# Constant matmuls at seven borders of a two-block network on one core, and one half of a weight split placed earlier

## The chip, the cores and the metric

The program runs on one core of a Trainium2 chip. The metric is device time in microseconds (us). Engines are named as in the profile: PE (TensorE, with PEld for its weight loads), DVE (VectorE), ACT (ScalarE), POOL (GpSimd), and SP, which issues the weight loads from memory. PE is granted one of two clocks, 2.4 or 1.2 GHz; the profile writes them as 1.00 and 0.50.

## The reference, cut to what matters

256 tokens of width 1024 go through a gated mixer block, a squared-relu feed forward, an RMS norm, and then two layers of a second block, each with gated feed forwards, an attention or a pooling mixer, and a layer norm after each part. All is float32. What this case touches is the norm between one part and the next:

```python
def rms_norm(x, w=None):
    xf = x.astype(jnp.float32)
    y = xf * lax.rsqrt(jnp.mean(jnp.square(xf), axis=-1, keepdims=True) + EPS)
...
def layer_norm(x, g, b):
    xf = x.astype(jnp.float32)
    mu = jnp.mean(xf, axis=-1, keepdims=True)
    var = jnp.mean(jnp.square(xf - mu), axis=-1, keepdims=True)
    y = (xf - mu) * lax.rsqrt(var + LN_EPS)
    return (y * g.astype(jnp.float32) + b.astype(jnp.float32)).astype(x.dtype)
...
    for i in range(DEPTH_2):
        x = layer_norm(DEEPNORM_ALPHA * x + 0.5 * swiglu(x, ffn_w_gu[i, 0], ffn_w_down[i, 0]), ...)
        ... y = moba_attention(x) or pool_mixer(x) ...
        x = layer_norm(DEEPNORM_ALPHA * x + y, ln_g[i, 1], ln_b[i, 1])
        x = layer_norm(DEEPNORM_ALPHA * x + 0.5 * swiglu(x, ffn_w_gu[i, 1], ffn_w_down[i, 1]), ...)
```

## The kernel before, in words

Activations lie transposed: 8 blocks of 128 channels by 256 tokens (`XS`, whose first half is called `xb` and holds x, and whose second half `sq` holds its squares). Each product is computed in three matmuls of a rounded format: the activation and the weight are each cut into a rounded part and a rest (`hi` and `lo`), and PE adds lo x hi, hi x lo and hi x hi (lines 601, 603 and 604 of the profile). `H` holds both parts of the normed x, one block of `H` is one step of the sum over channels.

Weights stream in panels of 128 x 2048 floats (1 MB), in the order in which they are used. SP loads a panel into one of four `raw` places. ACT copies each half of it, rounded, into `w_hi` (line 1104), and DVE subtracts it into `w_lo` (line 1504). These two together are called the split of a half panel. `w_hi` and `w_lo` have two places, so the split of a half waits until PE is through with the same half of the panel two before (`half_used`).

The program is written out per engine, in a fixed order; semaphores tie the engines. After the first, interwoven part come 17 stages, from `out` to `down3`. Eight of them end in a norm (`NORMED`): `out`, `ff2`, `down0`, `att_out`, `down1`, `down2`, `pool_out`, `down3`. What lies between such a stage and the first product of the next one is called a border here; seven have a next stage. At a border:

- The last four output banks are finished one by one. DVE takes each into x (`new_x`, line 1560, or 1565 where there is no mean), ACT squares it (1112), and DVE and POOL fold the blocks into `part` (1573, 567).
- PE sums over channels with a matrix of constant 1/1024 (`stats`, lines 747 to 757), mean first, then squares. ACT squares the mean (1174), DVE forms the variance (1618, 1619, or 1621 where there is no mean), ACT takes logarithm and exponential (1177, 1179), which gives the inverse root.
- Then for each of the 8 blocks: DVE subtracts the mean (`centred`, 1608), multiplies by the scale and the inverse root (`scaled`, 1636), ACT rounds it into `H` (1188, 1186), and DVE writes the rest (`lo`, 1644, 1642), which raises `norm_lo`.
- PE's next stage begins with its first group, 96 matmuls over 8 blocks: twelve for a block, which it may do as soon as that block's `norm_lo` is there (`ready`).

Two halves of the second panel of the next stage are split inside the border (`split_after`). Half 0: on ACT ahead of the logarithm, on DVE in `apply_norm` at m = 3, between the second block's rest and the fourth block's scaling. Half 1: on ACT after the fourth rounding, on DVE at m = 5.

Of the kernel before, what the change touches and what calls it, by code (L numbers as in the profile page):

```python
# [10 lines left out]
P = 128  # L11
T = 256
TT = T // P
D = 1024
KD = D // P
CHUNK = 512
PANEL = 4 * CHUNK
BANKS = 4
# [153 lines left out]
def two_blocks(nc, panels, x_in, c_in, cols_in, heads_in, ws_in, bs_in, wdt_in, rel_in, onehot_in, inv_in,  # L172
               skew, out):
    ctx = ExitStack()
    with ctx:
# [416 lines left out]
        def _(pe):  # L592
# [169 lines left out]

            def bias_rows(first, n):

                for h in range(first, first + n):
                    if h >= 2:
                        pe.wait_ge(S["rev_other" if h % 2 else "rev_copied"], h // 2)
                    to = banks[:, 1 + h % 2, :]
                    pe.matmul(to, rel_r[:, 0, h:h + 1].to_broadcast([33, P]), onehot_r[:, :], start=True, stop=False)
                    pe.matmul(to, rel_r[:, 1, h:h + 1].to_broadcast([33, P]), onehot_r[:, :], start=False, stop=True)\  # L770
                        .then_inc(S["rev_done"], 1)
# [203 lines left out]
            stats(2, False, "out")  # L975
            stage_k8("ff1", H, norm_block(1))
            stage_long("ff2", HH, 32, operand_of("ff1", 4))
            stats(3, False, "ff2")

            norm = [4]  # L980

            def feed_forward(i):
                stage_k8(f"gu{i}", H, norm_block(norm[0] - 2))
                stage_long(f"down{i}", HH, 22, operand_of(f"gu{i}", 2))
                stats(norm[0], True, f"down{i}")
                norm[0] += 1
# [80 lines left out]
            stats(norm[0], True, "att_out")  # L1067
            norm[0] += 1
# [4 lines left out]
            s = INDEX["pool_group"]  # L1073
# [16 lines left out]
            stats(norm[0], True, "pool_out")  # L1090
            norm[0] += 1
# [4 lines left out]
        def _(act):  # L1096
# [52 lines left out]
            def squares_post(s, g, G):  # L1149
                if by_bank(s, g):  # L1150
                    act.preload_act_table_set("natural_log_exp_and_others")
                    for b in range(BANKS):
                        square(s, g, b)
                    return
                act.wait_ge(taken, FIRST_GROUP[s] + g + 1)
                act.activation(by_group(sq)[:, g, :, :], by_group(xb)[:, g, :, :], ACT.Square)\
                    .then_inc(S["squares"], BANKS)
# [12 lines left out]
            def border_root(n, mean, stage_name):  # L1170
# [4 lines left out]
                split_after(split, stage_name, 0)  # L1175
# [309 lines left out]
        def _(vec):  # L1485
# [89 lines left out]
            def last_group(name, g, G, new_x):  # L1575

                for b in range(BANKS):
# [3 lines left out]
                    bank_post(INDEX[name], g, G, b, new_x)  # L1581

# [47 lines left out]
            def apply_norm(k, dest, scale, bias, stage_name, mean=False, operand=True):  # L1630
# [21 lines left out]
                for m in range(KD + 1):  # L1652
                    if m in (3, 5):
                        split_after(split, stage_name, m // 2 - 1)
# [490 lines left out]
```

## Time and profile before

| what | value |
|---|---|
| time, median of 3 runs | 1671.67 us (1669.38 to 1672.41) |
| the profiled execution: its own time | 1670.81 us |
| its span, first to last instruction | 1668.9 us |
| granted PE clock, mean | 0.968 |
| PE busy | 1584.6 us (95%) |
| DVE busy | 997.2 us (60%) |
| ACT busy | 770.9 us (46%) |
| POOL busy | 185.7 us (11%) |
| DMA queues, mean | 174 GB/s |

The span is 1.9 us shorter than the execution's own time, so what is read inside the span is set against 1670.81 and not against the median. A busy share of PE is not the share of its peak: matmuls overlap in the record, and at the lower clock PE is just as busy with half the work.

### The profile page before, as it was taken

How to read it: one execution, taken by the hardware profiler on the slowest of the kernel's cores; microseconds unless marked ns; L12 is line 12 of the kernel's file. 1: busy time of each engine (PE TensorE's matmuls, PEld its weight loads, DVE VectorE, ACT ScalarE, POOL GpSimd, SP SyncE). 2: the span in 40 equal slices, each digit the busy share in tenths (PEclk: the TensorE clock that was granted, in tenths of full speed). 3: DMA queues.
4: the chain of work that ended last, by engine and by line, in shares of the span. 5: the costliest groups of instructions: out<-in, count | busy, mean ns of one | idle time of the engine just before them, and what ended most of it. 6: DMA issues, size and time to landing. Idle time of an engine off the chain costs nothing.

```text
span 1668.9 us, 30136 instructions
## 1 busy us (share of the span) xinstructions
PE 1584.6 (95%) x12512; PEld 1534.6 (92%) x12512; DVE 997.2 (60%) x1278; ACT 770.9 (46%) x1006; POOL 185.7 (11%) x143
## 2 busy tenths in 40 slices
PE   7999999988999999999999879999999997799997
PEld 5999998878989999999989679999899997799997
DVE  5876894345766645655465655555655558565545
ACT  3544555444455534544443545443544444354433
POOL 0100002332110001000022012001200013120001
PEclk9999999989999999999999989999999998899999
DMA  8964763222535555455535325554455543344550
GB/s 316 368 246 165 292 229 124 102 77 102 185 145 179 191 185 177 163 190 176 187 141 189 114 79 200 178 194 181 151 179 187 190 177 127 126 152 176 180 192 32
DMA packets 42153, 289.66 MB, mean 174 GB/s; under 512 B 4843, under 2 KB 7019, under 8 KB 7500
## 3 DMA queue, kind: packets, MB, share of 16 engines
q1 hardware_dynamic: 41244, 284.44, 46.9%
q0 software_dynamic: 816, 3.87, 0.6%
q8 instruction: 72, 1.18, 0.3%
q14 instruction: 21, 0.17, 0.0%
HBM read 285.15 MB, written 3.15 MB: 173 GB/s over the span
## 4 chain that ended last, share of the span: by engine, by line
PE 86%; DVE 6%; ACT 3%; issue 2%; POOL 1%; DMA 1%; SPq 0%; ACTq 0%; POOLq 0%; DVEq 0%
PE banks L601 21%; PE banks L603 21%; PE banks L604 20%; PE banks L702 6%; PE banks L704 6%; PE banks L705 6%; DVE w_lo L1504 2%; ACT w_hi L1104 1%; POOL part L567 1%; PE banks L916 0%; PE banks L733 0%; PE banks L827 0%; DMA raw<-in_panels 0%; PE banks L919 0%; PE banks L826 0%
## 5 line engine op out<-in xcount | busy, mean ns | idle before, releaser
L1504 DVE TENSOR_TENSOR w_lo<-raw,w_hi 128x1024 fp32r<-128x1024 f32 x490 | 614.5, 1263 | 532.1 <-ACT w_hi L1104 526.9
L1104 ACT ACTIVATE w_hi<-raw 128x1024 fp32r<-128x1024 f32 x490 | 515.4, 1057 | 578.7 <-PE banks L604 421.4
L601 PE MATMUL banks<-H,w_lo 128*128 128x256 f32 x1920 | 549.5, 286 | 29.6 <-DVE H L1644 20.1
L603 PE MATMUL banks<-H,w_hi 128*128 128x256 f32 x1920 | 548.3, 286 | 0.0
L604 PE MATMUL banks<-H,w_hi 128*128 128x256 f32 x1920 | 546.6, 285 | 0.0
L601 PEld LDWEIGHTS banks<-H,w_lo 128*128 128x128 f32 x1920 | 368.7, 192 | 32.8 <-issue 32.3
L604 PEld LDWEIGHTS banks<-H,w_hi 128*128 128x128 f32 x1920 | 369.1, 192 | 0.0
L603 PEld LDWEIGHTS banks<-H,w_hi 128*128 128x128 f32 x1920 | 369.1, 192 | 0.0
L603 PE MATMUL banks<-HH,w_hi 128*128 128x256 f32 x960 | 270.8, 282 | 0.0
L601 PE MATMUL banks<-HH,w_lo 128*128 128x256 f32 x960 | 270.6, 282 | 0.0
L604 PE MATMUL banks<-HH,w_hi 128*128 128x256 f32 x960 | 270.1, 281 | 0.0
L702 PE MATMUL banks<-H,w_lo 128*128 128x256 f32 x640 | 188.3, 294 | 3.8 <-DVE H L1707 3.6
L704 PE MATMUL banks<-H,w_hi 128*128 128x256 f32 x640 | 185.4, 290 | 0.0
L705 PE MATMUL banks<-H,w_hi 128*128 128x256 f32 x640 | 185.1, 289 | 0.0
L604 PEld LDWEIGHTS banks<-HH,w_hi 128*128 128x128 f32 x960 | 181.0, 189 | 0.0
L603 PEld LDWEIGHTS banks<-HH,w_hi 128*128 128x128 f32 x960 | 180.8, 188 | 0.0
L601 PEld LDWEIGHTS banks<-HH,w_lo 128*128 128x128 f32 x960 | 180.7, 188 | 0.0
L702 PEld LDWEIGHTS banks<-H,w_lo 128*128 128x128 f32 x640 | 125.9, 197 | 6.4 <-issue 6.0
L704 PEld LDWEIGHTS banks<-H,w_hi 128*128 128x128 f32 x640 | 126.0, 197 | 0.0
L705 PEld LDWEIGHTS banks<-H,w_hi 128*128 128x128 f32 x640 | 125.7, 196 | 0.0
L567 POOL TENSOR_TENSOR part<-XS 128x512 f32<-128x512 f32 x8 | 10.3, 1289 | 904.4 <-issue 582.8
L1134 ACT ACTIVATE HH<-ev 128x512 f32 (+2 forms) x52 | 36.3, 698 | 80.6 <-DVE ev L1549 67.8
(285 smaller groups left out, 1706.5 us busy)
## 6 DMA issues: line engine op xcount, KB each, us to landing
raw<-in_panels SPq DMA_DIRECT2D x269, 1024.0 KB, 4.8
bias_rows<-rev POOLq DMA_DIRECT2D x1, 2048.0 KB, 16.9
XS<-in_x_t SPq DMA_DIRECT2D x1, 1024.0 KB, 6.6
near<-bias_rows POOLq DMA_DIRECT2D x8, 128.0 KB, 2.8
out_t<-XS SPq DMA_DIRECT2D x4, 256.0 KB, 2.6
ws<-in_ws_t POOLq DMA_DIRECT2D x1, 512.0 KB, 9.3
cols<-in_cols SPq DMA_DIRECT2D x1, 180.0 KB, 2.4
wdt<-in_wdt POOLq DMA_DIRECT2D x1, 128.0 KB, 5.9
```

The costliest lines, as they stand in the source:

```text
L567: pool.tensor_tensor(total, XS[:, 0, :, :] if b == 1 else total, XS[:, b, :, :], ALU.add)\
L601: pe.matmul(acc, w_lo[:, panel_slot, at:at + P], operand[:, kk, 0, :], start=starts and c == chunks[0], stop=False)
L603: pe.matmul(acc, w_hi[:, panel_slot, at:at + P], operand[:, kk, 1, :], start=False, stop=False)
L604: return pe.matmul(acc, w_hi[:, panel_slot, at:at + P], operand[:, kk, 0, :], start=False, stop=stops and c == chunks[-1])
L702: pe.matmul(acc, w_lo[:, q % SPLIT, at:at + P], operand[:, k, 0, :], start=p == 0 and c == 0 and b % 2 == 0, stop=False)
L704: pe.matmul(acc, w_hi[:, q % SPLIT, at:at + P], operand[:, k, 1, :], start=False, stop=False)
L705: last = pe.matmul(acc, w_hi[:, q % SPLIT, at:at + P], operand[:, k, 0, :], start=False, stop=p == panels - 1 and c == 3 and b % 2 == 1)
L1104: act.activation(w_hi[:, sl, w], raw[:, r, w], ACT.Copy).then_inc(panel_hi, 1)
L1134: act.activation(view[:, g, :, :], ev[:, G, 0:blocks, :], ACT.Copy).then_inc(operand_hi, 1)
L1504: vec.tensor_tensor(w_lo[:, sl, w], raw[:, r, w], w_hi[:, sl, w], ALU.subtract).then_inc(panel_lo, 1)
```

## The change

`keep_busy(n, bank)` issues n matmuls of 128 x 256 whose operands are constants (`ident_r`, the identity, and `never`, a mask of the first block of the network) into the fourth bank of the group just finished. Nothing reads that result. `busy_border(stage)` issues 24 of them at a border, in five pieces, each behind a wait: 6 after the sums, 7 once the variance is there, 4 once the inverse root is, 4 once the first block is scaled, 3 once it is rounded. It is called at the seven borders.

The split of half 0 moves, on both engines and at the same seven borders. ACT now does it ahead of squaring the last block of x. DVE now does it right after the last block of x has been formed, ahead of everything of the mean and the variance.

```diff
--- before.py
+++ after.py
@@ -760,6 +760,25 @@
                 pe.matmul(banks[:, b, T:2 * T], mean_w[:, :], sq[:, 0, :], start=True, stop=False)
                 pe.matmul(banks[:, b, T:2 * T], mean_w[:, :], sq[:, 1, :], start=False, stop=True)                    .then_inc(S["stat_sums"], 1)
 
+            def keep_busy(n, bank):
+
+                for _ in range(n):
+                    pe.matmul(banks[:, bank, 0:T], ident_r[:, :], never[:, :].unsqueeze(1).to_broadcast([P, 2, P]),
+                              start=True, stop=True)
+
+            def busy_border(stage):
+
+                k, bank = NORMED.index(stage) + 1, stat_bank(stage) + 3
+                keep_busy(6, bank)
+                pe.wait_ge(S["stat_var"], k + 2)
+                keep_busy(7, bank)
+                pe.wait_ge(S["stat_root"], k + 2)
+                keep_busy(4, bank)
+                pe.wait_ge(S["norm_y"], KD * k + 1)
+                keep_busy(4, bank)
+                pe.wait_ge(S["norm_hi"], KD * k + 1)
+                keep_busy(3, bank)
+
             def bias_rows(first, n):
 
                 for h in range(first, first + n):
@@ -973,9 +992,11 @@
                     group_sums(SSM_GROUPS - 1)
             stage_k8("out", MX, lambda k: pe.wait_ge(operand_lo, -(-k // 2)))
             stats(2, False, "out")
+            busy_border("out")
             stage_k8("ff1", H, norm_block(1))
             stage_long("ff2", HH, 32, operand_of("ff1", 4))
             stats(3, False, "ff2")
+            busy_border("ff2")
 
             norm = [4]
 
@@ -983,6 +1004,8 @@
                 stage_k8(f"gu{i}", H, norm_block(norm[0] - 2))
                 stage_long(f"down{i}", HH, 22, operand_of(f"gu{i}", 2))
                 stats(norm[0], True, f"down{i}")
+                if i < 3:
+                    busy_border(f"down{i}")
                 norm[0] += 1
 
             feed_forward(0)
@@ -1065,6 +1088,7 @@
             q = FIRST_PANEL[INDEX["att_out"]] + 3
             products(1 - att_group, q, q % SPLIT, AO, 4, False, True, each=bank_done)
             stats(norm[0], True, "att_out")
+            busy_border("att_out")
             norm[0] += 1
             feed_forward(1)
             feed_forward(2)
@@ -1088,6 +1112,7 @@
             last.then_inc(half_used, 2)
             stage_k8("pool_out", H, operand_of("pool_group", 4))
             stats(norm[0], True, "pool_out")
+            busy_border("pool_out")
             norm[0] += 1
             feed_forward(3)
 
@@ -1150,6 +1175,8 @@
                 if by_bank(s, g):
                     act.preload_act_table_set("natural_log_exp_and_others")
                     for b in range(BANKS):
+                        if b == BANKS - 1:
+                            split_after(split, STAGES[s][0], 0)
                         square(s, g, b)
                     return
                 act.wait_ge(taken, FIRST_GROUP[s] + g + 1)
@@ -1172,7 +1199,6 @@
                 if mean:
                     act.wait_ge(S["mean_sum"], n - 3)
                     act.activation(st[:, 3, :], banks[:, stat_bank(stage_name), 0:T], ACT.Square).then_inc(S["stat_mean"], 1)
-                split_after(split, stage_name, 0)
                 act.wait_ge(S["stat_var"], n + 1)
                 act.activation(st[:, 1, :], st[:, 1, :], ACT.Ln).then_inc(S["stat_log"], 1)
                 act.wait_ge(S["stat_log"], n - 1)
@@ -1579,6 +1605,7 @@
                         vec.wait_ge(S["norm_part"], 4 * NORMED.index(name) + 4)
                         add_block(name, 5)
                     bank_post(INDEX[name], g, G, b, new_x)
+                split_after(split, name, 0)
 
             def stage_x(name, new_x, biased=0):
 
@@ -1650,8 +1677,8 @@
                     centred(stage_name, 2)
                 vec.wait_ge(S["stat_root"], k + 2)
                 for m in range(KD + 1):
-                    if m in (3, 5):
-                        split_after(split, stage_name, m // 2 - 1)
+                    if m == 5:
+                        split_after(split, stage_name, 1)
                     if m < KD:
                         scaled(m)
                     if mean and m + 3 < KD:
```

On PE, from `out` to `ff1`, before (`never` and `ident_r` do not occur here):

```order
L753 MATMUL banks<-XS,mean_w 128x256 [waits squares,bank_x]
L755 MATMUL banks<-part,mean_w 128x256 [waits norm_whole]
L757 MATMUL banks<-XS,mean_w 128x256 [waits squares]
L601 MATMUL banks<-H,w_lo 128x256 [waits norm_lo,panel_lo,banks_taken]
L603 MATMUL banks<-H,w_hi 128x256
```

The same place now:

```order
L757 MATMUL banks<-XS,mean_w 128x256 [waits squares]
L766 MATMUL banks<-never,ident_r 128x256 x6
L766 MATMUL banks<-never,ident_r 128x256 [waits stat_var]
L766 MATMUL banks<-never,ident_r 128x256 x6
L766 MATMUL banks<-never,ident_r 128x256 [waits stat_root]
L766 MATMUL banks<-never,ident_r 128x256 x3
L766 MATMUL banks<-never,ident_r 128x256 [waits norm_y]
L766 MATMUL banks<-never,ident_r 128x256 x3
L766 MATMUL banks<-never,ident_r 128x256 [waits norm_hi]
L766 MATMUL banks<-never,ident_r 128x256 x2
L601 MATMUL banks<-H,w_lo 128x256 [waits norm_lo,panel_lo,banks_taken]
```

Between the last sum and the first product of the next stage stand 24 matmuls and four waits that were not there.

On DVE, from `down0` to `qk`, before (`w_lo` is the split, `H` the rest of a block, `norm_hi` ACT's rounding):

```order
L1560 SCALAR_TENSOR_TENSOR XS<-XS,banks 128x256 [waits half_used]
L1608 TENSOR_TENSOR XS<-XS,banks 128x256 [waits stat_mean]
L1618 SCALAR_TENSOR_TENSOR st<-banks,st 128x256 [waits stat_sums]
...
L1644 SCALAR_TENSOR_TENSOR H<-XS,cols,H 128x256 [waits norm_hi]
L1504 TENSOR_TENSOR w_lo<-raw,w_hi 128x1024 [waits panel_hi]
L1636 SCALAR_TENSOR_TENSOR XS<-XS,cols,st 128x256 [waits norm_centred]
L1608 TENSOR_TENSOR XS<-XS,banks 128x256
L1644 SCALAR_TENSOR_TENSOR H<-XS,cols,H 128x256 [waits norm_hi]
```

The same place now:

```order
L1586 SCALAR_TENSOR_TENSOR XS<-XS,banks 128x256 [waits half_used]
L1530 TENSOR_TENSOR w_lo<-raw,w_hi 128x1024 [waits panel_hi]
L1635 TENSOR_TENSOR XS<-XS,banks 128x256 [waits stat_mean]
L1645 SCALAR_TENSOR_TENSOR st<-banks,st 128x256 [waits stat_sums]
...
L1671 SCALAR_TENSOR_TENSOR H<-XS,cols,H 128x256 [waits norm_hi]
L1663 SCALAR_TENSOR_TENSOR XS<-XS,cols,st 128x256 [waits norm_centred]
L1635 TENSOR_TENSOR XS<-XS,banks 128x256
L1671 SCALAR_TENSOR_TENSOR H<-XS,cols,H 128x256 [waits norm_hi]
```

The `w_lo` instruction went from between two `H` writes to a place ahead of the first one that waits for `stat_mean`.

On ACT at the same border, before (`w_hi` is ACT's part of the split):

```order
L1112 ACTIVATE XS<-XS 128x256 [waits bank_x] x3
L1112 ACTIVATE XS<-XS 128x256 [waits banks_taken]
L1174 ACTIVATE st<-banks 128x256 [waits mean_sum]
L1104 ACTIVATE w_hi<-raw 128x1024 [waits half_used,panel_loaded_2]
L1177 ACTIVATE st<-st 128x256 [waits stat_var]
```

The same place now:

```order
L1137 ACTIVATE XS<-XS 128x256 [waits bank_x] x3
L1129 ACTIVATE w_hi<-raw 128x1024 [waits half_used,panel_loaded_2]
L1137 ACTIVATE XS<-XS 128x256 [waits banks_taken]
L1201 ACTIVATE st<-banks 128x256 [waits mean_sum]
L1203 ACTIVATE st<-st 128x256 [waits stat_var]
```

The `w_hi` instruction went from behind the squared mean to between the third and the fourth square.

## Rows read from the trace of the kernel before

**Rows 1.** Page, part 4: the chain that ended last, by engine

```profile
PE 86%; DVE 6%; ACT 3%; issue 2%; POOL 1%; DMA 1%; SPq 0%; ACTq 0%; POOLq 0%; DVEq 0%
```

**Rows 2.** Waits of PE: engine line, waited for, us in total, times, longest

```profile
PE banks L601 <- DVE H L1644: 20.1, 6, 3.4
```

**Rows 3.** Windows from `down0` to `qk`: from:to, length, busy by engine, PEclk, DMA share, GB/s

```profile
862.00:864.00 2.00, 0.00 (x0) 0.00 (x0) 1.49 (x5) 0.92 (x2) 0.00 (x0) 0.77 0.00 0
866.00:868.00 2.00, 2.00 (x11) 2.00 (x11) 2.00 (x4) 0.59 (x2) 0.00 (x0) 0.50 0.00 0
```

**Rows 4.** Timeline of PE, same border: start, length, line, instruction, idle before

```profile
860.14 0.59 PE L757 MATMUL banks<-XS,mean_w 128*128 128x256 f32 x2
864.14 0.55 PE L601 MATMUL banks<-H,w_lo 128*128 128x256 f32 x1 [3.41 <-DVE H L1644]
...
864.70 0.41 PE L604 MATMUL banks<-H,w_hi 128*128 128x256 f32 x1
864.92 0.41 PE L601 MATMUL banks<-H,w_lo 128*128 128x256 f32 x1
...
870.10 0.28 PE L603 MATMUL banks<-H,w_hi 128*128 128x256 f32 x1
870.22 0.27 PE L604 MATMUL banks<-H,w_hi 128*128 128x256 f32 x1
```

**Rows 5.** Windows: first group of 96 matmuls after each of seven borders; sum

```profile
478.30:492.38 14.08, 14.08 (x96) 14.08 (x97) 11.52 (x19) 7.25 (x11) 0.00 (x0) 0.79 0.29 101
...
864.14:878.16 14.02, 14.02 (x96) 14.02 (x97) 12.67 (x23) 7.37 (x11) 4.65 (x3) 0.79 0.27 86
...
1189.38:1202.55 13.17, 13.16 (x96) 12.91 (x97) 11.01 (x22) 8.74 (x13) 3.80 (x4) 0.87 0.22 81
...
sum 93.12, PE 93.11 PEld 92.69 DVE 79.45 ACT 55.91 POOL 19.23; mean PE 13.30 PEld 13.24 DVE 11.35 ACT 7.99 POOL 2.75
```

**Rows 6.** Timeline of DVE, from `down0` to `qk`

```profile
859.89 0.42 DVE L1608 TENSOR_TENSOR XS<-XS,banks 128x256 f32<-128x256 f32 x1 [1.64 <-ACT st L1174]
...
863.51 0.48 DVE L1644 SCALAR_TENSOR_TENSOR H<-XS,cols,H 128x256 fp32r<-128x256 f32 x1 [0.24 <-ACT H L1188]
...
865.37 0.48 DVE L1644 SCALAR_TENSOR_TENSOR H<-XS,cols,H 128x256 fp32r<-128x256 f32 x1
865.76 1.22 DVE L1504 TENSOR_TENSOR w_lo<-raw,w_hi 128x1024 fp32r<-128x1024 f32 x1
866.90 0.48 DVE L1636 SCALAR_TENSOR_TENSOR XS<-XS,cols,st 128x256 f32<-128x256 f32 x1
...
867.62 0.48 DVE L1644 SCALAR_TENSOR_TENSOR H<-XS,cols,H 128x256 fp32r<-128x256 f32 x1
...
870.67 0.48 DVE L1644 SCALAR_TENSOR_TENSOR H<-XS,cols,H 128x256 fp32r<-128x256 f32 x1
```

**Rows 7.** Timeline of ACT, same border

```profile
856.86 0.42 ACT L1112 ACTIVATE XS<-XS 128x256 f32<-128x256 f32 x1 [1.00 <-DVE XS L1560]
858.29 0.42 ACT L1112 ACTIVATE XS<-XS 128x256 f32<-128x256 f32 x1 [1.01 <-DVE XS L1560]
...
859.76 1.05 ACT L1104 ACTIVATE w_hi<-raw 128x1024 fp32r<-128x1024 f32 x1
```

**Rows 8.** Timeline of DVE, from `ff2` to `gu0`, a border without a mean

```profile
665.18 0.42 DVE L1621 TENSOR_SCALAR st<-banks 128x256 f32<-128x256 f32 x1 [1.24 <-PE banks L757]
```

**Rows 9.** Window inside the attention, columns as in rows 3

```profile
924.00:944.00 20.00, 18.03 (x91) 14.28 (x91) 12.97 (x38) 9.31 (x24) 0.00 (x0) 1.00 0.31 109
```

**Rows 10.** Waits of PE from 920 to 970 us, in the attention

```profile
PE banks L1039 <- DVE probs L1999: 3.6, 5, 1.3
```

**Rows 11.** Timeline of PE in the first part: the constants' matmul, and the next

```profile
300.40 0.38 PE L919 MATMUL banks<-never,ident_r 128*128 128x256 f32 x1
300.71 0.38 PE L916 MATMUL banks<-cum_r,ident_r 32*128 32x256 f32 x1
```

**Rows 12.** Timeline of DVE after `down1`: first split for `gu2`'s second group

```profile
1200.63 1.48 DVE L1504 TENSOR_TENSOR w_lo<-raw,w_hi 128x1024 fp32r<-128x1024 f32 x1 [1.98 <-ACT w_hi L1104]
```

## The prediction, as put on record

> **What bounds the kernel now.** First the chain of waits: the work that ended last runs through PE for 86% of the span [rows 1]. Only what shortens PE's own sequence can change the time by much. Second the waits of PE: where it waits longest in total, it is the first product of a stage that waits for DVE's rest of the first normed block, six times 3.4 us [rows 2]. That is the border, and the change works there and nowhere else. Third, the windows over one border: while PE is idle its granted clock falls within 862 to 864 us, and it is 0.50, the 1.2 GHz level, while PE is busy without a break again [rows 3] (a mean of 0.77 over two us puts the fall at 863.1). Fourth PE's timeline there: the last sum starts at 860.14 (two passes, ending at 860.73), the first product at 864.14, after 3.41 us idle. From then on a matmul starts 0.22 us after the one before, later 0.12 us [rows 4]; by the two clocks, 256 columns at 1.2 GHz are 0.213 us, and for the full clock I use 0.119, the same rows over a longer stretch. So a border costs the idle time, and then a first group at half pace. Fifth, the first group of 96 matmuls at each of the seven borders: 14.08, 14.02, 13.17 us and so on, 93.12 us in sum, at mean clocks of 0.79 to 0.89 [rows 5]. At 0.119 us for a matmul it would be 11.4 us each, 79.8 us for seven. Thus 13.3 us lie above the full pace, and that is all the change can reach, unless the idle time itself shrinks. It does not: the chain to the first block's rest (sums, variance, logarithm, exponential, scaling, rounding, rest) keeps its instructions.
>
> **The filler matmuls.** Added are 7 x 24 matmuls of 128 x 256. Their price, if nothing hides them, is 168 x 0.12 = 20 us. What hides them is the idle time: from the end of the last sum's issue (some 0.2 us ahead of 860.73) to 864.14 there are 3.6 us, and 24 x 0.12 = 2.9 us. They come in five pieces, each released by a step of the chain, so the last piece counts: three matmuls behind the rounding of the first block. DVE's rest of that block starts at 863.51, released by that rounding, and ends at 863.99; PE's product follows 0.15 later [rows 4, 6]. A filler piece released by the same rounding can start at about 863.63 by the same 0.15, and three matmuls with one weight load ahead are through by 864.1. That ends against the 864.14 of the product, with nearly nothing to spare. I put 0.05 us for a border, 0.35 in all. Behind the waiting fillers stands only the first group, which waits for a later step of the same chain anyway.
>
> The price of one filler is bounded by two rows. Matmuls of this size in a row start 0.12 apart [rows 4]; the same matmul, constants and all, is followed by the next one after 0.31 us in the first part [rows 11]. There it stands between matmuls that use 32 rows of the array, so a weight load cannot be hidden; in the border the fillers stand among their like, as the products of rows 4 do. I take 0.12, and keep 0.31 for a rival.
>
> Does PE keep its full clock on them? The trace has no such filling. Its nearest place is the attention: PE waits there up to 1.3 us at a time [rows 10], and its clock is 1.00 throughout [rows 9]. Between the pieces of fillers I count gaps of 0.5 us at most. So I take it that the clock holds. The Trainium skill speaks against that in "TensorE: Matmul & The Clock Gate", section "A second HAM failure mode: psum-queue depth-cycling": a PE that idles briefly between groups of matmuls can swing between its two levels. By that rule the sum would be that of rival 1; the trace agrees in part, for the attention has such short idling and no fall [rows 9, 10].
>
> **The moved split of half 0.** At `down0` DVE's part stands at 865.76, is 1.22 long, and the next instruction starts at 866.90: it holds back everything from the third block's rest on by 1.14 us. Second rest ends at 865.85, third at 868.10 (867.62 + 0.48), fifth at 871.15 [rows 6].
> - Its new place on ACT: the third square ends at 857.28, the fourth starts at 858.29, after 1.01 us idle [rows 7]. The half of the weights that is overwritten is free six matmuls (0.7 us) before the stage's last, whose end at 857.8 starts the last block of x; so at 857.1. ACT's 1.05 us then reach from 857.28 to 858.33, and the square is late by 0.05 at most. That square is summed last, so at a border with a mean it is hidden wholly.
> - Its new place on DVE: idle for 1.64 us until 859.89 [rows 6]. From 858.38 on, 1.22 us end at 859.60, 0.29 before the wait for the squared mean is over. At a border without a mean the hole is 1.24 us [rows 8], just as long: up to 0.1 late at two borders. I cost both at 0.
> - What it gives: the third block and all after it are ready 1.14 us earlier. At the low clock this is worth nothing, since twelve matmuls at 0.213 take 2.56 us and PE comes to the third block after DVE. At the full clock it decides.
>
> **What is late next, and the sum.** At the full clock twelve matmuls take 1.42 us. First block at 864.14; second ready at 865.85, so PE starts it at 865.90, 1.76 after the first, and not 1.42. Third: ready at 866.96 with the split moved, PE comes at 867.32: no wait. Fifth: ready at 870.01, PE comes at 870.17: no wait. So the group takes 1.76 + 84 x 0.119 = 11.76 us instead of 14.02. With this length at all seven (the two borders without a mean are a little shorter) they take 82.3 us instead of 93.1: 10.8 us gained. Less 0.35 for the fillers: 10.4 us. After that PE must find the next group's weights split. The tightest row is after `down1`: the first half is there at 1202.11 (1200.63 + 1.48) [rows 12], and the group ended at 1202.55 [rows 5]. Both move, DVE's by 1.14 and the group's end by 1.41, to 1200.97 and 1201.14: still in time, so nothing is given back.
>
> Against the profiled execution's own 1670.81 us that makes 1660.4; against the median of the runs, 1671.67, 1661.3. I say 1661.0. Alone, by the same steps, the fillers would give about half: PE waits for the third block, ready at 868.10, so a group takes 4.01 + 72 x 0.119 = 12.6 us, seven take 88, and 5 us are gained. The moved split alone gives nothing.
>
> **Rivals.**
> 1. The fillers do not count, and the clock falls as before. For it: no row shows fillers; against it: rows 9 and 10. Then the groups keep their 93.1 us, the moved split gives nothing, and the last seven fillers at 0.213 us take 1.5 us from about 863.1 on: the first product comes at 864.6 instead of 864.14, 0.45 x 7 = 3.2 us later. 1674.0. The Trainium skill has a rule of this kind for transposes ("TensorE: Matmul & The Clock Gate", "Part 4: PE-mode transpose": they do not count as PE being busy in the same way); the fillers load an identity but are plain matmuls, and no run here shows which.
> 2. The slow side: a filler costs what it costs in the first part, 0.31 us [rows 11]. 24 x 0.31 = 7.4 us do not fit into 3.6 us, each border's first product is 3.9 us late, 27 us in all, less the 13.3 of the pace: 1685. It decides from 0.22 us a filler on (24 x 0.22 = 5.3, late by 1.7, 12 us in all, which eats the gain). Against it: only the row between matmuls of 32 rows says so.
> 3. The split ahead of the mean holds up the variance: its panel lands late, or `half_used` comes late, and ACT's part does not fit the 1.01 us. Each us of delay in the chain is a us for PE. For it: the hole without a mean is no longer than the work [rows 8]; against it: 0.29 us of room with a mean [rows 6, 7]. With half a us at each border, 3.5 us: 1664.5; with all of the 1.14 at each, 8.0 us: 1669.
>
> **How the numbers follow.** Forecast 0.74, rival 1 0.11, rival 2 0.06, rival 3 0.09. The forecast's own range is 1657.5 (all 13.3 us) to 1664 (fillers held at some borders only, or a before whose clock fell less often in the timed runs). With rival 3 taken in and the two slow rivals left out, 1657 to 1667. This kernel's runs can tell a difference of about 0.2%, 3.3 us. Faster by more: forecast and most of rival 3, 0.83. Within: part of rival 1, 0.07. Slower by more: rival 2 and the rest of rival 1, 0.10.
>
> **What the profile of the changed kernel would show.** Right: clock 1.00 in the windows of the borders, fillers 0.12 us apart, the first product still 0.15 us behind the first block's rest and some 3.4 us behind the last sum, the first groups at 11.4 to 11.8 us, the moved split inside DVE's wait for the squared mean, the third rest 1.1 us earlier. Wrong: a clock of 0.50 after a border (rival 1), fillers more than 0.2 us apart and a first product that waits for PE itself (rival 2), the first block's rest later behind the stage's last product than before (rival 3), or a wait for split weights at the end of the first group, which would be the gain given back.

## The result, and the profile after

| | before | after |
|---|---|---|
| median | 1672.04 us (1669.38 to 1672.52, 4 runs) | 1654.7 us (1652.84 to 1658.67, 4 runs) |
| the profiled execution, its span | 1668.9 us | 1654.4 us |
| granted PE clock, mean | 0.968 | 0.977 |

The ratio is 0.9903, with an interval of 0.988 to 0.9926, which is 16.2 us of 1672.04. The kernel is faster, as forecast, but its median is 6.3 us below the forecast of 1661.0 and 2.3 us below the range. A second timing of both gave 1655.63 against 1668.95, a ratio of 0.9924 (0.99 to 0.9947), which is 12.7 us.

The first groups of the seven borders, of the changed kernel. They answer to [rows 5].

```profile
477.10:488.57 11.47, 11.47 (x98) 11.47 (x98) 10.29 (x18) 7.20 (x11) 0.00 (x0) 1.00 0.26 94
...
858.83:870.67 11.84, 11.74 (x98) 11.54 (x98) 11.20 (x22) 7.25 (x11) 3.61 (x3) 1.00 0.26 90
...
1180.58:1192.41 11.83, 11.74 (x97) 11.53 (x97) 9.67 (x21) 8.60 (x13) 3.60 (x4) 1.00 0.26 90
...
sum 82.08, PE 81.61 PEld 80.58 DVE 70.48 ACT 55.59 POOL 18.03; mean PE 11.66 PEld 11.51 DVE 10.07 ACT 7.94 POOL 2.58
```

The clock is 1.00 in all seven, and the sum is 82.08 us, where 82.3 was forecast and 93.12 stood before. PE's timeline at the border after `down0`, against [rows 4]:

```profile
854.82 0.59 PE L757 MATMUL banks<-XS,mean_w 128*128 128x256 f32 x2
855.06 3.77 PE L766 MATMUL banks<-never,ident_r 128*128 128x256 f32 x24
858.83 0.36 PE L601 MATMUL banks<-H,w_lo 128*128 128x256 f32 x1
...
860.59 0.39 PE L601 MATMUL banks<-H,w_lo 128*128 128x256 f32 x1
...
862.12 0.28 PE L601 MATMUL banks<-H,w_lo 128*128 128x256 f32 x1
```

The 24 constant matmuls fill what was 3.41 us of idle time. The second block starts 1.76 us after the first, as worked out, and the third at 862.12. DVE and ACT at the same border, against [rows 6, 7]:

```profile
852.95 1.23 DVE L1530 TENSOR_TENSOR w_lo<-raw,w_hi 128x1024 fp32r<-128x1024 f32 x1
854.57 0.42 DVE L1635 TENSOR_TENSOR XS<-XS,banks 128x256 f32<-128x256 f32 x1 [0.40 <-ACT st L1201]
...
858.20 0.48 DVE L1671 SCALAR_TENSOR_TENSOR H<-XS,cols,H 128x256 fp32r<-128x256 f32 x1 [0.24 <-ACT H L1214]
...
861.18 0.47 DVE L1671 SCALAR_TENSOR_TENSOR H<-XS,cols,H 128x256 fp32r<-128x256 f32 x1
```

```profile
851.87 1.05 ACT L1129 ACTIVATE w_hi<-raw 128x1024 fp32r<-128x1024 f32 x1
852.97 0.42 ACT L1137 ACTIVATE XS<-XS 128x256 f32<-128x256 f32 x1
```

DVE's moved split ends 0.40 us before its next work is released. The first rest ends at 858.68, 0.15 before the product that it releases. The third rest starts 2.98 us after the first; before it was 4.11 (867.62 less 863.51). The window in which the clock fell, at 0.77 in [rows 3], is now:

```profile
857.00:859.00 2.00, 2.00 (x16) 1.82 (x15) 1.62 (x5) 0.61 (x2) 0.00 (x0) 1.00 0.00 0
```

The chain that ended last runs through PE as before, against [rows 1]:

```profile
PE 86%; DVE 7%; ACT 3%; issue 2%; POOL 1%; DMA 1%; SPq 0%; ACTq 0%; POOLq 0%; DVEq 0%
```

The first groups account for 11.0 of the 14.5 us between the spans. 1.2 us more lie ahead of all this: the first product of `ff1` starts at 477.10 and not at 478.30, though its own border is as long as before. 2.0 us lie in the last two stages, `gu3` and `down3`, behind the first group. There neither clock nor waits differ, yet in 50 us PE starts four matmuls fewer in the kernel before (first row) than in the changed one (second row):

```profile
1500.00:1550.00 50.00, 50.00 (x419) 50.00 (x418) 26.59 (x26) 23.20 (x28) 0.00 (x0) 1.00 0.49 178
```

```profile
1490.00:1540.00 50.00, 50.00 (x423) 50.00 (x423) 27.25 (x28) 23.63 (x27) 0.00 (x0) 1.00 0.54 189
```

By the starts in the trace a matmul follows the last one after 120.0 ns in the one and 118.7 ns in the other. I call them the slow and the normal pace. A stream of some 1560 matmuls, which is what two such stages have, is 2.0 us longer at the slow pace.

### The profile page after: what moved, and what is told of

Same layout as the page of the kernel before. It is cut to its first block, busy times and chain, and to the rows that moved or that the text cites. A ratio compares the mean times of both kernels' runs of the same rounds, so it can differ in the third digit from the quotient of the medians.

```text
span 1654.4 us, 30472 instructions
## 1 busy us (share of the span) xinstructions
PE 1593.1 (96%) x12680; PEld 1541.8 (93%) x12680; DVE 998.4 (60%) x1278; ACT 770.4 (47%) x1006; POOL 183.5 (11%) x143
## 4 chain that ended last, share of the span: by engine, by line
PE 86%; DVE 7%; ACT 3%; issue 2%; POOL 1%; DMA 1%; SPq 0%; ACTq 0%; POOLq 0%; DVEq 0%
PE banks L601 20%; PE banks L604 20%; PE banks L603 20%; PE banks L702 6%; PE banks L705 6%; PE banks L704 6%; DVE w_lo L1530 2%; ACT w_hi L1129 1%; POOL part L567 1%; PE banks L935 1%; DVE XS L1663 1%; PE banks L846 1%; PE banks L952 0%; PE banks L938 0%; PE banks L733 0%
## 5 line engine op out<-in xcount | busy, mean ns | idle before, releaser
L601 PEld LDWEIGHTS banks<-H,w_lo 128*128 128x128 f32 x1920 | 362.6, 189 | 9.2 <-issue 7.7
L603 PEld LDWEIGHTS banks<-H,w_hi 128*128 128x128 f32 x1920 | 362.7, 189 | 0.0
L604 PEld LDWEIGHTS banks<-H,w_hi 128*128 128x128 f32 x1920 | 362.6, 189 | 0.0
L702 PEld LDWEIGHTS banks<-H,w_lo 128*128 128x128 f32 x640 | 125.7, 196 | 6.3 <-issue 5.1
L704 PEld LDWEIGHTS banks<-H,w_hi 128*128 128x128 f32 x640 | 125.7, 196 | 0.0
L705 PEld LDWEIGHTS banks<-H,w_hi 128*128 128x128 f32 x640 | 125.3, 196 | 0.0
```

The costliest lines, as they stand in the source:

```text
L601: pe.matmul(acc, w_lo[:, panel_slot, at:at + P], operand[:, kk, 0, :], start=starts and c == chunks[0], stop=False)
L603: pe.matmul(acc, w_hi[:, panel_slot, at:at + P], operand[:, kk, 1, :], start=False, stop=False)
L604: return pe.matmul(acc, w_hi[:, panel_slot, at:at + P], operand[:, kk, 0, :], start=False, stop=stops and c == chunks[-1])
L702: pe.matmul(acc, w_lo[:, q % SPLIT, at:at + P], operand[:, k, 0, :], start=p == 0 and c == 0 and b % 2 == 0, stop=False)
L704: pe.matmul(acc, w_hi[:, q % SPLIT, at:at + P], operand[:, k, 1, :], start=False, stop=False)
L705: last = pe.matmul(acc, w_hi[:, q % SPLIT, at:at + P], operand[:, k, 0, :], start=False, stop=p == panels - 1 and c == 3 and b % 2 == 1)
```

## The experiments

**Each half alone, and the kernel before again.** The first takes the moved split back on both engines. The second leaves the split moved and the constants out:

```diff
             def busy_border(stage):
 
                 k, bank = NORMED.index(stage) + 1, stat_bank(stage) + 3
+                return
                 keep_busy(6, bank)
```

Expected of the constants alone: 

> The fillers at the seven borders, the split of half 0 left where it was. The theory that the borders add up as in the prediction: clock 1.00 in the seven first groups, but PE waits for the third block, which the split holds back, so the groups take about 12.6 us each, 88 in sum (before 93.1, changed kernel 82.1): 5 us faster than before from the borders. The rival that the moved split has no part in it: groups of 11.8 us, 11 us faster. On what the sum left out, the pace of the steady stream (118.7 or 120.0 ns from matmul to matmul): if a clock change in the middle of a stream is what can put it at 120, none of the long stages behind the first part runs at 120 here, and the whole is 5 to 8 us faster than before; if it is chance at any start of a stream, some may.

Expected of the split alone: 

> Half 0 of the split moved on ACT and DVE, no fillers. The sum of the prediction: nothing gained (ratio 1.000, at most 0.5 us), since at 1.2 GHz twelve matmuls take 2.56 us and PE comes to the third block after DVE anyway; the clock still falls at the seven borders and the first groups keep about 93 us. The rival that the split is worth 1.1 us at every border by itself: 8 us, ratio 0.995. That the split holds the variance up: slower by up to 3 us. The pace of the long stages may be 118.7 or 120.0 ns, as before.

Expected of the kernel before: 

> The kernel before, unchanged, for a second profile of it. The theory of the pace: at least one of the long stages behind a border at which the clock came back in the middle of the stream shows 120.0 ns instead of 118.7, which costs 2.0 us in a stage of 1500 matmuls; which stage differs from profile to profile. The rival that the last stage is slow for a reason of its own in this kernel: again the last stage, and only it. First groups 88 to 97 us in sum, by where the clock's falls lie.

Constants alone: 1663.32 us against 1670.7, ratio 0.9951 (0.9934 to 0.9969). Its first groups:

```profile
sum 88.97, PE 84.69 PEld 81.42 DVE 77.40 ACT 55.39 POOL 17.85; mean PE 12.10 PEld 11.63 DVE 11.06 ACT 7.91 POOL 2.55
```

The clock is held, and PE now waits for the third block behind the split that was not moved. PE's and then DVE's timeline of this kernel:

```profile
865.13 0.36 PE L601 MATMUL banks<-H,w_lo 128*128 128x256 f32 x1 [0.66 <-DVE H L1669]
```

```profile
862.64 1.22 DVE L1529 TENSOR_TENSOR w_lo<-raw,w_hi 128x1024 fp32r<-128x1024 f32 x1
...
864.50 0.48 DVE L1669 SCALAR_TENSOR_TENSOR H<-XS,cols,H 128x256 fp32r<-128x256 f32 x1
```

Split alone: 1669.66 us, ratio 0.9996 (0.9976 to 1.0016), first groups 92.89 us:

```profile
sum 92.89, PE 92.78 PEld 92.45 DVE 75.62 ACT 56.57 POOL 24.58; mean PE 13.25 PEld 13.21 DVE 10.80 ACT 8.08 POOL 3.51
```

So the constants bring about 4 to 5 us in these groups, the split nothing by itself, and 6.9 us (88.97 less 82.08) once the clock is held. In the times the constants alone gave 7.4 us, more than the 5 of the prediction.

Without constants the clock falls at most borders, but not at all of them. In the split alone the first group after `down1` has the full clock, and so has the one after `down2` in the third profile of the kernel before, which comes further down:

```profile
1183.07:1194.90 11.83, 11.73 (x97) 11.53 (x97) 9.67 (x21) 8.60 (x13) 3.60 (x4) 1.00 0.24 90
```

```profile
1385.78:1398.70 12.92, 12.16 (x96) 11.65 (x97) 12.27 (x23) 7.25 (x11) 3.56 (x3) 1.00 0.25 82
```

The five profiles without constants, all told, have 35 first groups, and these two are the only ones at the full clock. In the seven profiles with constants over the whole wait it is 49 of 49.

The kernel before once more took 1668.18 us, with 94.31 us in the first groups. Its slow stream lay elsewhere, in the stages `gu2` and `down2`, and its last two stages ran at the normal pace: the slow pace belongs to no stage.

**More constants in other holes.** Four holes outside the borders were filled too: ahead of `out`, between the sums after the attention, and two in the pool.

```diff
+            pe.wait_ge(S["y_skip"], PAIRS)
+            keep_busy(18, 7)
             stage_k8("out", MX, lambda k: pe.wait_ge(operand_lo, -(-k // 2)))
...
+                        if stage == "att_out":
+                            keep_busy(40, b + 2)
                         pe.wait_ge(taken, FIRST_GROUP[INDEX[stage] + 1])
...
+            pe.wait_ge(taken, FIRST_GROUP[s] - 1)
+            keep_busy(36, BANKS * (FIRST_GROUP[s] % 2) + 3)
             pe.wait_ge(panel_lo, 2 * (FIRST_PANEL[s] + 1))
...
+            pe.wait_ge(taken, FIRST_GROUP[s] + 1)
+            keep_busy(16, BANKS * (FIRST_GROUP[s] % 2) + 3)
             stage_k8("pool_out", H, operand_of("pool_group", 4))
```

Expected: 

> The changed kernel with fillers in four more idle stretches of PE: 18 ahead of the stage out (idle 2.4 us), 40 inside the sums of att_out (5.2 us), 36 ahead of pool_group (4.9 us), 16 ahead of pool_out once the first half of pool_group is taken (6.5 us). If the clock falls only where PE idles, the falls at 452, 978, 1401 and maybe 1415 us go. Worth by their stretches: about 1.7 us at out, 1.3 at att_out (its sums run at half pace), 0 ahead of pool_group (DVE is late there), up to 2.5 at pool_out: 3 to 5.5 us under the changed kernel. If fillers there are in the way of the chain, no gain.

1652.53 us, ratio 0.9897 (0.9871 to 0.9922). That is under the changed kernel's two ratios, but the intervals overlap, so the 3 to 5.5 us are not shown. The falls ahead of `out` and after the attention are gone; in the pool the clock still falls, and that part is 1.0 us longer. After the attention the clock fell in all twelve profiles without constants there and in neither of the two with them. Ahead of `out` nothing is shown: in three profiles without constants there (constants alone, first piece alone, and the kernel before for the third time) it did not fall either. The first two holes were then timed alone, beside the changed kernel.

Expected of the changed kernel again: 

> The changed kernel, unchanged, for its time beside the others and a second profile. The first groups of the seven borders take 82 us in sum again, no border at the low clock. Theory (the borders give 11 us, and some 3 us more come from elsewhere, mostly from long streams of matmuls that no longer run at 120.0 ns a matmul instead of 118.7): median 1654 to 1657 us, and fewer than 500 matmuls at 120.0 ns behind 480 us. Rival (only the borders gain, the first four runs were lucky): median 1659 to 1661.

Expected of the two holes: 

> The changed kernel with two more holes filled: 18 constant matmuls ahead of the stage out and 40 between the sums after the attention; the pool's holes, whose fillers cost 1 us in the earlier run and held nothing, are left alone. Theory: the clock stays up at both places, the border after the attention is 1.5 us shorter, the start of out some 1 us, and nothing is lost in the pool: 1651.5 to 1653.5, that is 2 to 3 us under the changed kernel in the same call. Rival (the low clock at these places cost nothing, the earlier run was under the changed one by luck): within 1 us of the changed kernel.

1655.63 us for the changed kernel, 1655.36 for the two holes (ratio to before 0.9911, 0.9885 to 0.9937). The changed kernel came in as its theory had it. Of the two holes the 2 to 3 us do not show in the times, which are 0.3 us apart, as the rival had it. The trace shows a part of them: from the first product of `ff1` to the end the profile with the two holes filled takes 1174.9 us (1653.1 less 478.21), that of the changed kernel run beside it 1177.1 (1649.6 less 472.46). Of these 2.2 us the border after the attention has 1.4, from last product to first 11.6 us instead of 13.0, close to the 1.5 that its theory had; 0.8 lie in the pool, where the two kernels are the same. Its own first product came 5.8 us later, which in this pair of profiles hides all of it. Between the sums after the attention PE waits in the changed kernel:

```profile
PE banks L749 <- DVE XS L1586: 5.2, 1, 5.2
```

With the two holes filled, PE's timeline there, and a window behind the wait:

```profile
973.75 5.14 PE L768 MATMUL banks<-never,ident_r 128*128 128x256 f32 x40
979.43 0.70 PE L751 MATMUL banks<-XS,mean_w 128*128 128x256 f32 x2 [0.55 <-DVE XS L1590]
```

```profile
980.00:982.00 2.00, 2.00 (x12) 1.79 (x11) 1.04 (x3) 0.38 (x1) 0.00 (x0) 1.00 0.00 0
```

And the same stretch of the first profile of the changed kernel, at a clock of 0.63 with eight matmuls instead of twelve:

```profile
980.00:982.00 2.00, 2.00 (x8) 1.59 (x6) 0.42 (x1) 0.38 (x1) 0.00 (x0) 0.63 0.00 0
```

**How many constants, and where.** Three kernels leave some of them out. One keeps the first piece alone, one half of each piece, one the last three pieces (excerpts of the three diffs; the remarks behind # are not in the kernels):

```diff
                 keep_busy(6, bank)        # first piece alone: the rest is gone
-                pe.wait_ge(S["stat_var"], k + 2)
-                keep_busy(7, bank)
...
-                keep_busy(6, bank)        # half of each: 3, 3, 2, 2, 2
+                keep_busy(3, bank)
...
-                keep_busy(6, bank)        # last three pieces: 4, 4, 3
                 pe.wait_ge(S["stat_var"], k + 2)
-                keep_busy(7, bank)
```

Expected of the first piece alone: 

> The changed kernel with only the first piece of constant matmuls at each border, the 6 behind the sums; PE is idle for some 2.7 us again after them. Theory (the clock stays only while PE has work in the whole chain): the clock falls at most borders, the first groups take 90 to 93 us, and the time is that of the moved split alone, 1667 to 1670. Rival (a little work is enough, or it only puts the fall off): first groups 82 to 86 us, 1655 to 1660.

Expected of half: 

> The changed kernel with 3, 3, 2, 2 and 2 constant matmuls in the five pieces instead of 6, 7, 4, 4 and 3: 12 in place of 24, none of the gaps between them over 1 us. Theory (short gaps are enough, as in the attention, where PE waits up to 1.3 us and keeps its clock): clock 1.00 at all seven borders, first groups 82 us, first products no earlier than with 24, time within 1 us of the whole change. Rival (the share of busy time in the border counts): the clock falls at some or all of the borders, first groups 85 to 93 us, 1658 to 1669.

Expected of the last three: 

> The changed kernel without the first two pieces (6 behind the sums, 7 behind the variance): only the 11 behind the inverse root, the first scaling and the first rounding, so PE is idle for some 2 us first. Theory (12 spread over the whole chain were enough, the 6 of its start alone at three borders of seven; what counts is that the idle stretch is short, wherever it lies): the clock holds at most borders, first groups 82 to 86 us. Rival (it falls in the idle stretch, and the fillers then run at half clock): first groups 88 to 93 us.

Half: 1656.91 us, ratio 0.9927 (0.9906 to 0.9947), first groups 82.08 us, clock 1.00 in all: twelve do what 24 do. The time is 1.3 us above the changed kernel's, not within 1 us, but the two ratios are 0.9924 and 0.9927. First piece alone: 1662.37 us, ratio 0.9964 (0.9945 to 0.9983), first groups 86.69 us: the clock holds in three groups of seven (after `out`, `down1`, `down2`). Neither theory had that. Last three alone, one run: 1658.84 us, first groups 85.0 us, as its theory had it; it holds in four (after `ff2`, `down0`, `down1`, `down2`). Its rival has a part too. After the attention the clock had fallen, the constants ran at half pace, and the first product came late, 4.3 us behind the last sum instead of 3.4:

```profile
983.86 2.69 PE L766 MATMUL banks<-never,ident_r 128*128 128x256 f32 x11 [1.83 <-ACT st L1203]
986.35 0.42 PE L601 MATMUL banks<-H,w_lo 128*128 128x256 f32 x1
```

With part of the idle time left open the clock holds at some borders and not at others. The longest idle stretch does not tell them apart: in the first piece alone it falls after 2.2 us at one border and holds after 2.7 at others. Each kernel was profiled once, so how much of this belongs to the border and how much is chance stays open. Where it falls with the first piece alone, at `ff2`, PE's timeline and the windows show:

```profile
659.26 1.06 PE L766 MATMUL banks<-never,ident_r 128*128 128x256 f32 x6
662.54 0.55 PE L601 MATMUL banks<-H,w_lo 128*128 128x256 f32 x1 [2.22 <-DVE H L1661]
```

```profile
662.00:664.00 2.00, 1.46 (x7) 1.49 (x8) 1.91 (x5) 0.81 (x2) 0.00 (x0) 0.50 0.00 0
664.00:666.00 2.00, 2.00 (x13) 2.00 (x13) 1.64 (x5) 1.67 (x3) 0.00 (x0) 0.65 0.00 0
700.00:750.00 50.00, 50.00 (x419) 50.00 (x418) 27.64 (x28) 22.76 (x27) 0.00 (x0) 1.00 0.49 178
```

From the rise of the clock at 665.4 on the stream is at the slow pace, 419 matmuls in 50 us.

**The price of a constant matmul.** Twelve instead of three in the last piece:

```diff
                 pe.wait_ge(S["norm_hi"], KD * k + 1)
-                keep_busy(3, bank)
+                keep_busy(12, bank)
```

Expected: 

> The changed kernel with 12 constant matmuls in the last piece of each border, the one behind the first block's rounding, in place of 3. Theory (a constant matmul costs the same 0.119 us as a product's, and the three of the change just fit): the 12 take 1.42 us from some 0.5 us ahead of the product's old start, so each first product is 0.9 to 1.0 us later, 6.3 to 7.5 us in all, less up to 0.34 for each border, since the second block is then ready when the first one's twelve are through; first groups 11.4 us. Rival (a constant matmul costs 0.31 us in a row as in the first part): each first product 3.2 us later.

One run, 1660.91 us. DVE's first rest, PE's first product, and the first groups:

```profile
860.03 0.48 DVE L1671 SCALAR_TENSOR_TENSOR H<-XS,cols,H 128x256 fp32r<-128x256 f32 x1 [0.25 <-ACT H L1214]
```

```profile
861.59 0.28 PE L601 MATMUL banks<-H,w_lo 128*128 128x256 f32 x1
```

```profile
sum 79.86, PE 79.86 PEld 79.86 DVE 67.60 ACT 52.37 POOL 20.55; mean PE 11.41 PEld 11.41 DVE 9.66 ACT 7.48 POOL 2.94
```

The rest ends at 860.51, and 0.15 later the product could start; it starts at 861.59, 0.93 late. Nine more constants at 0.119 are 1.07 us, so the three of the change had 0.14 us to spare. The borders together, from the last product of a stage to the first of the next, are 7.0 us longer, the first groups 2.2 us shorter. The theory holds and 0.31 us apiece is out.

**Where the rest of the gain comes from.** Two more profiles without constants, of the kernel before and of the moved split alone.

Expected: 

> The kernel before, unchanged, a third profile for the pace of its matmul streams. Theory (a clock that rises in the middle of a stream of matmuls now and then leaves it at 120.0 ns a matmul instead of 118.7, till the stream ends): each stream of over 300 matmuls at 120.0 ns begins within a us of the end of a stretch at the low clock. Rival (the pace is drawn at the start of a stage): such a stream begins at a first product with the clock long up. First groups 93 to 94.5 us; a stage of 1500 matmuls at the slow pace is 2.0 us longer.

Expected: 

> The moved split alone once more, for the same question and for the first product of ff1, which came between 471.9 and 478.3 us in the profiles so far. By the theory streams at 120.0 ns begin where the clock rises within them, and with seven more such rises than in the changed kernel one profile in two or so has one; by the rival they begin at first products. First groups 92 to 94 us, first product of ff1 anywhere from 472 to 478 us, since nothing ahead of it differs.

1669.53 and 1674.91 us, one run each. The first groups took 95.1 and 94.2 us, both a little over their ranges, and the first product of `ff1` in the second came at 480.34, outside of its range. In the second, two streams ran at the slow pace. The windows show the rise of the clock, the slow stream behind it, and a stage before it at the normal pace (424):

```profile
1194.00:1196.00 2.00, 2.00 (x11) 2.00 (x11) 2.00 (x4) 1.12 (x2) 0.00 (x0) 0.50 0.00 0
1196.00:1198.00 2.00, 2.00 (x19) 2.00 (x18) 2.00 (x6) 1.02 (x2) 0.00 (x0) 0.97 0.38 49
...
1200.00:1250.00 50.00, 50.00 (x419) 50.00 (x418) 28.60 (x27) 24.10 (x29) 10.02 (x8) 1.00 0.52 180
...
1000.00:1050.00 50.00, 50.00 (x424) 50.00 (x423) 30.61 (x34) 25.81 (x31) 10.27 (x8) 1.00 0.53 189
```

All profiles side by side, behind the first product of `ff1`; a slow stream is one of over 300 matmuls at 120.0 ns, "lost" is what its stages take above their usual length, and the last column is the span less the start of `ff1`:

| profile | first groups, us | slow streams | lost, us | `ff1` starts at | from there to the end, us |
|---|---|---|---|---|---|
| before | 93.1 | 1 | 2.0 | 478.30 | 1190.6 |
| before, second | 94.3 | 1 | 2.0 | 475.54 | 1190.7 |
| before, third | 95.1 | 1 | 0.4 | 477.39 | 1190.2 |
| split alone | 92.9 | 0 | 0 | 471.95 | 1187.4 |
| split alone, second | 94.2 | 2 | 4.0 | 480.34 | 1192.6 |
| first piece alone | 86.7 | 2 | 2.4 | 475.37 | 1184.9 |
| last three pieces | 85.0 | 0 | 0 | 475.26 | 1181.6 |
| constants alone | 89.0 | 0 | 0 | 477.91 | 1184.6 |
| changed | 82.1 | 0 | 0 | 477.10 | 1177.3 |
| changed, second | 82.1 | 0 | 0 | 472.46 | 1177.1 |
| half | 82.1 | 0 | 0 | 473.57 | 1177.3 |
| four holes more | 82.2 | 1 | 0.4 | 478.21 | 1177.4 |
| two holes more | 82.1 | 0 | 0 | 478.21 | 1174.9 |
| twelve last | 79.9 | 1 | 0.4 | 478.05 | 1180.9 |

The seven slow streams of kernels whose clock falls at some border all begin where a stretch at the low clock ends (1467.2, 1191.5, 868.8, 1196.1, 1472.6, 665.4 and 863.4 us; seven of 60 such ends). That is the theory's side. But the two in kernels that hold the clock at the borders begin within 2 us of the first product of `qk`, with the clock at 1.00: a fall isn't the only way in, so the rival has a part too. What sets the pace is not shown.

The last column leaves the first part out. It repeats within 0.5 us in the three profiles of the kernel before and within 0.2 in the two of the changed one, and the difference of their means is 13.3 us.

## Why the prediction was right in kind and too small

- **The clock holds on constants**: right, 1.00 at all seven borders, 82.08 us of first groups for a forecast 82.3. Rival 1 falls. The Trainium skill's "TensorE: Matmul & The Clock Gate", section "A second HAM failure mode: psum-queue depth-cycling", tells of a kernel whose clock swings because PE idles briefly between groups of matmuls. Idling of up to 0.5 us between the pieces, in the kernel with half of the constants, did not bring the clock down here. Its section "Part 4: PE-mode transpose" is about transposes, and the constants are none: these plain matmuls with the identity as the weight hold the clock, and no run here tries transposes in their place.
- **Their price**: 0.05 us for a border was put down; it was nothing, with 0.14 us to spare. From the last sum's end to the first product it is 3.41 us before and 3.42 now. By their starts in the trace the constants of a piece follow each other after 0.12 us, but for the first pair of the first piece (0.31) and of the second (0.22). Rival 2 falls by the run with twelve.
- **The moved split**: free in its new place. At borders with a mean DVE has 0.40 us to spare. At one without, DVE's split stands just ahead of the variance and touches it:

```profile
660.14 1.22 DVE L1530 TENSOR_TENSOR w_lo<-raw,w_hi 128x1024 fp32r<-128x1024 f32 x1
661.37 0.42 DVE L1648 TENSOR_SCALAR st<-banks 128x256 f32<-128x256 f32 x1
```

  Yet the time from the end of `ff2` to the next first product is 4.66 us in both kernels, so rival 3 falls. The feared wait for `gu2`'s weights [rows 12] did not come either: the group behind `down1` is among the 11.83s.
- **The halves alone**: 5 us and nothing were forecast. In the groups it was 4.2 and 0.2 against the first profile, and 5.2 and 0.6 with the mean of the profiles of each kernel. The constants' groups took 12.93 us where there is a mean, not 12.6: the third block came 4.10 us after the first instead of 4.01, and the fifth late once more.
- **The step that failed** is the sentence that the 13.3 us above the full pace are "all the change can reach", with the 10.8 us of the sum that was taken out of them, and so the lower end of 1657. Behind the first product of `ff1` the change is worth 13.3 us by the last column of the table, where 10.4 were forecast; that the two 13.3 are the same number is chance. Two things lay outside of the sum. First, the 93.12 us came from one profile; the kernel before took 94.3 and 95.1 in two others, so the groups give 12.1 us in the mean (94.2 less 82.1), and not 10.8. Second, the pace of the streams behind the border, which the sum did not have at all: five profiles with no constants lost 1.7 us to it in the mean, the seven whose clock held at all seven borders lost 0.1. Together 13.7 us, a ratio of 0.9918. That lies in both measured intervals; the forecast's 10.4 (0.9938) lies in the second alone.
- **What was left out of the range** is chance in the first part: the same instructions reach the first product of `ff1` between 471.95 and 480.34 us.

```profile
471.95 0.55 PE L601 MATMUL banks<-H,w_lo 128*128 128x256 f32 x1 [3.08 <-DVE H L1672]
```

```profile
480.34 0.55 PE L601 MATMUL banks<-H,w_lo 128*128 128x256 f32 x1 [3.09 <-DVE H L1672]
```

  Both rows are of the split alone. The length of the first part goes with the time at the low clock in it, by the windows of the same two profiles up to these rows:

```profile
0.00:471.95 471.95, 445.15 (x3370) 411.47 (x3371) 315.45 (x447) 227.49 (x338) 76.83 (x74) 0.97 0.54 201
```

```profile
0.00:480.34 480.34, 454.36 (x3370) 420.34 (x3371) 314.60 (x447) 227.67 (x338) 76.90 (x74) 0.94 0.53 197
```

  The mean clock is 0.97 in the one and 0.94 in the other; by the trace that is 31 and 59 us at the low clock. Over all 14 profiles the first product comes about 0.3 us later for each us at the low clock ahead of it (correlation 0.92). What makes the clock fall more often in one execution than in another stays open.

  23 runs of the kernel before lay between 1662.4 and 1677.36 us, five times the width that the three shown had. So a median of four can be some us off on each side, and luck has a part in the miss: 13.3 us less than the 1671.67 of before would be 1658.4, inside the range. The first comparison's 16.2 us and the second's 12.7 lie on either side of 13.3 and 13.7. Over all the timings, 41 runs of the kernel before and ten of the changed one, the medians are 15.2 us apart. That the 2 us above 13.3 are the first part's spread is argued from its size, not shown by a run of its own.

## What to carry to other kernels

Where a short chain of other engines stands between two long streams of matmuls, count not only PE's idle time but the group behind it at the low clock; matmuls on constants in the idle time cost nothing as long as the clock is up and the last piece ends before the real work is released, and half as many may do, if they are spread over the whole wait. Take the edits together and apart: the earlier split was worth nothing while the clock fell and 6.9 us once it held. Before setting a range, ask how far one profile stands for others: here the first part, which the change doesn't touch, differed by 8.4 us between two profiles of one kernel.

## What the hardware showed that was not expected

- A steady stream of these matmuls has two paces at the same granted clock of 1.00, 118.7 and 120.0 ns (424 or 423 against 419 in 50 us). It keeps one up to the end of the stream, for as long as 189 us here.
- Twelve constants in five pieces held the clock at every border, six or eleven on one side of the idle time at three and four of seven. With none the first group had the full clock at two of 35 borders.
- The first part of one and the same kernel took 471.95 us with 31 us of it at the low clock, and 480.34 with 59.
